# The beginning of a two-layer attention kernel: input rows normalised in groups of four, a second buffer for the modulated rows, and another order of modulation and low part

## What is computed

```python
shift, scale, gate = split(silu(c) @ a_ada_w + a_ada_b, 3)      # one vector c of 1024
u = rms_norm(x, a_norm_g) * (1 + scale) + shift
q, k, v, z = split(u @ a_w_in, 4)                               # 1024 x 4096
q, k = rms_norm per half head of 64
o = (softmax_1(q1 k1) - lam * softmax_2(q2 k2)) @ v             # causal, ALiBi, 8 heads
h = x + gate * ((rms_norm(o) * silu(z)) @ a_w_out)
... # shared k, v from h; then layer 1 the same way with a window of 128
```

## Time and profile before

| | |
|---|---|
| median of 3 runs | 1270.98 us (1269.91 to 1271.34) |
| profiled execution | 1269.83 us, of which the span of the trace is 1268.0 us |
| mean granted TensorE clock | 0.972 of full speed |
| busy: TensorE, VectorE, ScalarE, GpSimd | 91%, 57%, 53%, 14% of the span |
| mean traffic | 85 GB/s |

### The profile page before, as it was taken

One profiled execution on the slowest core, in us unless ns is written; L12 is line 12 of the kernel. 1 busy time (PEld: TensorE's weight loads), 2 busy tenths in 40 slices (PEclk: granted clock), 3 DMA queues, 4 the chain that ended last, 5 costly groups with the idle time before them and its releaser, 6 DMA issues.

```text
span 1268.0 us, 19274 instructions
## 1 busy us (share of the span) xinstructions
PE 1153.3 (91%) x6048; PEld 895.4 (71%) x6048; DVE 724.8 (57%) x2307; ACT 666.6 (53%) x2037; POOL 172.5 (14%) x305
## 2 busy tenths in 40 slices
PE   0657999999999999999996999869999999997998
PEld 0545677777777777777764888758878878786886
DVE  6446667676766677676765354545555545555221
ACT  2356566565656555565654455546666666664110
POOL 3121111110101111010110111031111111110122
PEclk9989999999999999999997999979999999997999
DMA  9411122132222223232224233210111111123342
GB/s 366 168 46 57 55 89 93 64 97 70 84 78 75 86 70 92 69 93 71 90 63 140 96 109 111 68 58 22 48 41 39 39 50 38 42 58 123 116 133 83
DMA packets 52390, 107.42 MB, mean 85 GB/s; under 512 B 5824, under 2 KB 18240, under 8 KB 51264
## 3 DMA queue, kind: packets, MB, share of 16 engines
q1 hardware_dynamic: 52288, 106.18, 26.2%
HBM read 89.38 MB, written 16.78 MB: 84 GB/s over the span
## 4 chain that ended last, share of the span: by engine, by line
PE 81%; DVE 7%; issue 5%; ACT 4%; DMA 2%; POOL 1%; SPq 0%; POOLq 0%; DVEq 0%; ACTq 0%
PE ps_p L512 14%; PE ps_p L514 13%; PE ps_p L513 13%; PE ps_s L544 6%; PE ps_o L591 5%; PE ps_p L690 4%; PE ps_p L691 4%; PE ps_p L692 4%; PE ps_o L659 3%; PE ps_t L615 3%; PE ps_s L643 2%; PE ps_t L675 2%; PE ps_o L714 2%; DVE adabuf L1388 1%; PE ps_o L606 1%
## 5 line engine op out<-in xcount | busy, mean ns | idle before, releaser
L512 PE MATMUL ps_p<-w_hi,u_hi 128*128 128x512 f32 x768 | 338.9, 441 | 0.0
L514 PE MATMUL ps_p<-w_hi,u_lo 128*128 128x512 f32 x768 | 305.4, 398 | 0.0
L513 PE MATMUL ps_p<-w_lo,u_hi 128*128 128x512 f32 x768 | 304.5, 396 | 0.0
L512 PEld LDWEIGHTS ps_p<-w_hi,u_hi 128*128 128x128 f32 x768 | 147.4, 192 | 64.0 <-ACT gbuf L781 28.6
L514 PEld LDWEIGHTS ps_p<-w_hi,u_lo 128*128 128x128 f32 x768 | 146.4, 191 | 33.4
L513 PEld LDWEIGHTS ps_p<-w_lo,u_hi 128*128 128x128 f32 x768 | 148.0, 193 | 17.8
L826 ACT ACTIVATE e<-e,negm 128x256 f32<-128x256 f32 (+7 forms) x128 | 98.2, 768 | 97.9 <-DVE negm L1101 96.9
L1000 DVE TENSOR_TENSOR w_lo<-raw,w_hi 128x512 fp32r<-128x512 f32 x120 | 81.8, 690 | 99.7 <-ACT w_hi L754 99.7
L448 POOL TENSOR_SCALAR gbuf<-gbuf 128x128 f32<-128x128 f32 (+1 forms) x96 | 37.3, 388 | 580.4 <-ACT gbuf L781 580.4
L544 PE MATMUL ps_s<-kT,qT 64*128 64x512 f32 (+3 forms) x384 | 89.4, 542 | 6.4 <-DVE negm L1101 5.4
L754 ACT ACTIVATE w_hi<-raw 128x512 fp32r<-128x512 f32 x128 | 79.3, 629 | 25.0 <-DMA raw<-w_a 19.1
(11 more groups left out here) (169 smaller groups left out, 2051.5 us busy)
## 6 DMA issues: line engine op xcount, KB each, us to landing
adabuf<-ada_w SPq DMA_DIRECT2D x64, 384.0 KB, 3.3
raw<-w_a SPq DMA_DIRECT2D x80, 256.0 KB, 3.5
raw<-w_b SPq DMA_DIRECT2D x48, 256.0 KB, 3.1
ada_in<-ada_w SPq DMA_DIRECT2D x7, 1024.0 KB, 13.2
x_in<-x SPq DMA_DIRECT2D x8, 512.0 KB, 11.9
oa_scratch<-gbuf SPq DMA_DIRECT2D x64, 64.0 KB, 1.6
e<-oa_scratch SPq DMA_DIRECT2D x8, 512.0 KB, 3.9
stage<-x SPq DMA_DIRECT2D x8, 512.0 KB, 5.4
```

The costliest lines, as they stand in the source:

```text
L512: pe.matmul(o, u_hi[:, c, t], w_hi[par][:, c, :], start=(c == 0), stop=False)
L513: pe.matmul(o, u_hi[:, c, t], w_lo[par][:, c, :], start=False, stop=False)
L514: mm = pe.matmul(o, u_lo[:, c, t], w_hi[par][:, c, :], start=False, stop=(c == KD - 1))
```

## The change

The loads of x for tiles 1 to 3 are issued earlier: tile 1 behind tile 0, tiles 2 and 3 between the modulation weights. The groups are ((0, 4), (4, 8)): tiles 0 to 3 are squared before the weight chunks 4 to 7 are split on ScalarE, and VectorE makes their root and normalises all four after the fourth of its weight steps. TensorE transposes tiles 0 and 1 ahead of the sums. `u_mod` gets two buffers, over `oT`, which is used only by the output projections; so tile n waits for the low part of tile n-2. Tiles 0 and 1 are both modulated before the first slot. In the slots, VectorE modulates the next tile right behind the head's normalisation instead of at the slot's end, and makes the low part of tile i at the end of slot i instead of at its start. The memset of `oss`, for which TensorE's first wait (`s_const`) counts, moves to the beginning. GpSimd's normalisations move one slot later. All eight products of the first modulation remain on VectorE and its sums on TensorE.

```diff
         x_in = over(w_at, "x_in", [P, 2, KD, FW])
+        oT_at = nc.sbuf_base + (-nc.sbuf_base) % 32
         oT = sb("oT", [P, 2, D], F32R)
+
+        u_mod = over(oT_at, "u_mod", [P, 2, D])
...
-        x_groups = ((0, 1), (1, 2), (2, 4), (4, 8))
+        ada0_sum = ps_p[:, 0, :]
+
+
+        x_groups = ((0, 4), (4, 8))
...
             load_x(0)
+            load_x(1)
             for c in range(RAW):
                 load_chunk(0, c, w_a[0, :, c, :])
             for c in range(KD - 1):
                 sp.dma_start(ada0_in[:, c, :], ada0_w[c]).then_inc(ada0_loaded[c], 16)
+                if c in (1, 3):
+                    load_x(2 + c // 2)
...
-            for n in range(1, NT):
+            for n in range(4, NT):
                 load_x(n)
...
+                    if is_a and u == 0 and 2 <= i < 5:
+
+                        if i == 2:
+                            pool.wait_ge(n_rs, 2)
+                        for n in ((4, 5), (6,), (7,))[i - 2]:
...
                     part_of_projection(range(0, 3))
-                    if i:
-                        next_rows(0)
+                    next_rows(0)
+                    if i < 3:
+                        next_rows(1)
...
-                    if i:
+                    if i >= 3:
                         next_rows(1)
...
-            rows_of_x(0, 0)
-            rows_of_x(0, 1)
+            for n in range(2):
+                rows_of_x(n, 0)
+                rows_of_x(n, 1)
...
             def x_modulate(n):
                 act.wait_ge(n_tr, 2 * n + 2)
-                at_least(act, u_ready, n)
+                at_least(act, u_ready, n - 1)
...
-                    if isinstance(u, int) and u == 0 and i < NT - 1:
+                    if isinstance(u, int) and u == 0 and 1 <= i < NT - 1:
                         x_modulate(i + 1)
-                        if i < 2:
-                            for n in range(*x_groups[i + 2]):
+                        if i == 1:
+                            for n in range(*x_groups[1]):
                                 x_squares(n)
-                            x_seed(i + 2)
+                            x_seed(1)
...
-            x_squares(0)
+            for n in range(*x_groups[0]):
+                x_squares(n)
             x_seed(0)
...
+            act.wait_ge(s_mod0, 5)
             x_modulate(0)
-            x_squares(1)
-            x_seed(1)
+            x_modulate(1)
...
                 dve.wait_ge(n_tr, 2 * n + 1)
-                at_least(dve, u_ready, n)
-                modulate(x_transposed(n, 0), lambda d: u_mod[:, d * P:(d + 1) * P], 0, M_A_SHIFT, n_umod_d)
+                at_least(dve, u_ready, n - 1)
...
-                    if first and i:
-                        x_low(i)
...
                     if live(2):
                         head_norm(S, s, i2)
+                    if first and 1 <= i < NT - 1:
+                        x_modulate(i + 1)
+                        if i == 1:
+                            x_roots(1)
...
                     split_for(u, i, par, live, units, U_A)
-                    if first and i < NT - 1:
-                        x_modulate(i + 1)
-                        if i == 0:
-                            x_roots(2)
-                            x_normalise(2, 2)
-                        elif i == 1:
-                            x_normalise(2, 3)
-                            x_roots(3)
+                    if first and i >= 2:
+                        x_low(i)
...
             dve.memset(ones[:, :], 1.0)
+            dve.memset(oss[:, :], 0.0).then_inc(s_const, 1)
             dve.memset(var[:, :], 1.0).then_inc(s_const, 1)
...
-            x_roots(0)
-            x_normalise(0, 0)
             acc = adabuf[:, 0:ADA0]
...
+            def ada0(c, step, t, j):
                 dve.wait_ge(ada0_loaded[c], 16)
-                if c == 0:
-                    dve.tensor_scalar(acc, ada0_in[:, 0, :], csil[:, 0:1], None, ALU.mult).then_inc(ada0_used, 1)
-                else:
-                    dve.wait_ge(ada0_used, min(c, KD - 1))
-                    dve.scalar_tensor_tensor(out=acc[:, t], in0=ada0_in[:, j, t], scalar=csil[:, j:j + 1],
-                                             in1=acc[:, t], op0=ALU.mult, op1=ALU.add).then_inc(ada0_used, 1)
-            dve.memset(oss[:, :], 0.0).then_inc(s_const, 1)
+                at_least(dve, ada0_used, min(step, KD - 1))
+                dve.scalar_tensor_tensor(out=acc[:, t], in0=ada0_in[:, j, t], scalar=csil[:, j:j + 1],
+                                         in1=acc[:, t], op0=ALU.mult, op1=ALU.add).then_inc(ada0_used, 1)
+
+            dve.wait_ge(ada0_loaded[0], 16)
+            dve.tensor_scalar(acc, ada0_in[:, 0, :], csil[:, 0:1], None, ALU.mult).then_inc(ada0_used, 1)
+            for c in range(1, KD - 1):
+                ada0(c, c, slice(0, ADA0), c)
+                if c == 3:
+                    x_roots(0)
+                    for n in range(*x_groups[0]):
+                        x_normalise(0, n)
+            for k in range(2):
+                ada0(KD - 1 + k, KD - 1 + k, slice(k * ADA0 // 2, (k + 1) * ADA0 // 2), KD - 1)
...
             x_modulate(0)
             x_low(0)
-            x_roots(1)
-            x_normalise(1, 1)
+            x_modulate(1)
+            x_low(1)
```

More of the change, by code:

```diff
@@ L194, in build @@
         ada_mm = sem("ada_mm")
+        s_mod0 = sem("s_mod0")
         s_mod = sem("s_mod")
@@ L437, in slot @@
                     i2, i3 = (i - 2) % 8, (i - 3) % 8
-                    if is_a and u == 0 and 1 <= i < 4:
-                        if i == 1:
-                            pool.wait_ge(n_rs, 4)
-                        for n in ((4, 5), (6,), (7,))[i - 1]:
+                    if is_a and u == 0 and 2 <= i < 5:
+                        if i == 2:
+                            pool.wait_ge(n_rs, 2)
+                        for n in ((4, 5), (6,), (7,))[i - 2]:
                             pool.tensor_scalar(x_rows(n), x_rows(n), xrs[:, n:n + 1], 1.0, ALU.mult,
@@ L560, in next_rows @@
                     def next_rows(half):
-                        if first and i < NT - 1:
+                        if first and 1 <= i < NT - 1:
                             rows_of_x(i + 1, half)
-                    if first and i == 0:
-                        next_rows(0)
-                        next_rows(1)
                     if live(3):
@@ L742, in _ @@
                 for j in range(k * 8, k * 8 + 8):
-                    mm = pe.matmul(ps_p[:, 0, j:j + 1], adabuf[:, j * P:(j + 1) * P], ones[:, :], start=True, stop=True)
+                    mm = pe.matmul(ada0_sum[:, j:j + 1], adabuf[:, j * P:(j + 1) * P], ones[:, :], start=True, stop=True)
                 mm.then_inc(ada0_mm, 1)
@@ L810, in x_modulate @@
                 act.wait_ge(n_tr, 2 * n + 2)
-                at_least(act, u_ready, n)
+                at_least(act, u_ready, n - 1)
                 for d in range(4, KD):
-                    last = act.activation(u_mod[:, d * P:(d + 1) * P], x_transposed(n, 1)[:, (d - 4) * P:(d - 3) * P],
+                    last = act.activation(u_mod[:, n % 2, d * P:(d + 1) * P], x_transposed(n, 1)[:, (d - 4) * P:(d - 3) * P],
                                           ACT.Identity, scale=smod[:, 0, d:d + 1],
```

30 lines of the change are left out of this document (12 added, 18 removed).

## The result

The changed kernel takes 1250.61 us (1250.21 to 1250.95, 4 runs); the kernel before took 1270.45 (1267.02 to 1271.34, 4 runs) beside it. The ratio is 0.9845 [0.9829, 0.9861]. The gain of 1.4 to 1.7% is clear of the noise, its sign and place are those of the prediction, and it is 1.5 us of span larger than the 17.3 forecast.

The account below looks back on a forecast made before the run. TensorE's own work bounds the kernel after about 135 us, so only earlier standstill can be won: 10.65 + 6.7 = 17.3 us off the profiled 1269.8 gives 1252.5, median 1253.6; range 1250.5 to 1256.5, wider 1250.0 to 1259.0.

Parts of the forecast that it names:

- The start of the modulation: Beginning: first modulation at 45.45 against 42.86, a loss of 2.6 us, since VectorE's weight steps wait for x3 and normalisations.
- The turns: Beginning: VectorE's half steps and GpSimd's splits of chunks 4 to 7 alternate, one split of 1.1 us before each half.
- My lower bound for that case: Beginning, without VectorE and GpSimd alternating: halves end at 37.0 and 38.3, sums at 43.8, 1.4 us later than before.
- First projection: Beginning: TensorE starts it at 49.35 instead of 50.35, no longer queued behind tile 1's transposes.
- The wait at 77.91: TensorE's wait before tile 0's q and k transposes: ends at 68.8, 9.1 us earlier, with some 7 us of standstill left.
- First scores: End of the early part: 10.65 us ahead, with tile 3's transposes half done and the 0.98 us modulation wait covered.
- Slots 3 to 7: VectorE's new order shortens TensorE's waits: 1.85 + 2.05 + 0.85 + 0.8 + 1.2 = 6.7 us gained.
- The loop with the output row as its second gate: From slot 5, q and k transposes also wait for the output row, behind the modulation: period 10.95 us instead of 9.3.
- Rival (a): Only the early gain comes; slots keep 11 to 12 us because TensorE waits for moved VectorE work: 1260.3 us, chance 0.12.
- Rival (b): Early part worse by more GpSimd alternation, or TensorE's low clock costing some 1.6 us per stretch: 1257 us, chance 0.1.
- Rival (c): Beginning: x3's load finishes last, at 41.3 us, holding VectorE; modulation 20 us later, 1273.6 us in all, chance 0.03.
- Rival (d): Whole kernel: nothing measurable, the gain lost again to some later wait; chance 0.01.

Follow-up runs that it names:

- the row-first kernel: Changed kernel, but VectorE's modulation of the next tile stands behind the output row instead of ahead of it: 1248.76 us, ratio 0.9832.
- the kernel without turns: Changed kernel, but GpSimd splits weight chunks 4 to 7 only after VectorE's last half step: 1250.73 us, ratio 0.9846.
- the early squares: Changed kernel, but ScalarE squares tiles 4 to 7, and both engines make their root, ahead of the first modulation: 1244.39 us, ratio 0.9794.
- the beginning alone: Changed kernel with VectorE's old order in the slots (low part at the start, next tile's modulation at the end): 1259.03 us, ratio 0.9908.
- the slots alone: Kernel before, with only the modulation moved forward in slots 2 to 6, low part still at the slot's start: 1270.58 us, ratio 1.0005.
- the later normalisations: Changed kernel, but VectorE normalises tiles 2 and 3 behind its last half step instead of behind the fourth step: 1248.67 us, ratio 0.9838.

## Why the prediction held, step by step

The forecast was 1253.6 and the kernel took 1250.61. Of the 3.0 us, 1.5 is span (18.8 gained, not 17.3). The rest is that I had set the median 1.2 above the profiled execution, and the changed kernel's lies 0.3 below its own. The measured time lies only 0.1 inside the narrower range of 1250.5 to 1256.5. The 1.5 of span is made of errors of both signs: 0.7 too much for the beginning, 0.5 too little for the slots, and 1.7 behind slot 7's start that no term stood for.

- **The start of the modulation: right in kind, 0.6 too small.** Forecast 45.45, measured 46.08. x3's load landed in its turn, 1.1 us later than I had summed (23.9, not 22.8). That wait was part of the chain; the normalisations, at 2.74, were cheaper than the 3.05. The turns were somewhat smaller than I had put them: 1.83 by the kernel without them, where the two splits of 1.1 make 2.2. Late start and smaller turns nearly cancel, and so the halves ended at 38.53 and 40.72 against 38.1 and 40.5. That it is turns, and not a slower VectorE, the kernel without them shows. My lower bound for that case had the sums 1.2 us earlier than the middle value; they moved by 0.87, and the two ends of the range were further apart than the mechanism allows.
- **First projection: 49.35 forecast, 50.05 measured,** the same 0.6 passed on and 0.1 more.
- **The wait at 77.91: 9.1 forecast, 8.2 measured.** Root ready at 64.68 instead of 63.2: 0.7 from above, 0.15 from the nine matmuls, and 0.6 from tile 2's eight transposes, which took 1.91 us in the slow clock where I had put 1.3. That is this execution's clock: with the same instructions up to there they took 1.03 in the kernel with the low part at the slot's start. The step behind it took 5.0 where I had put 5.5 (64.68 to 69.68). That the squares hold this wait is shown by their early version.
- **First scores: 10.65 ahead forecast, 9.93 measured.**
- **Slots 3 to 7: 6.7 forecast, 7.2 measured** (17.1 ahead at 117.60, less 9.9). Step for step: no wait in slot 3 (forecast none), 0.67 (0.65), 2.18 and 2.11 (some 2.1), 1.46 (1.1). The loop with the output row as its second gate was the right model: the row-first kernel takes 1.3 out of each of the two slots.
- **The single waits of the slots, in part luck.** The own work of 8.2, 8.7 and 9.3 belongs to slots 4, 5 and 6, one slot later than the prediction has the first two; a period of 9.3 would then leave 1.1 in slot 4, and one of 10.95 would leave 1.65 in slot 6. The periods came out as 8.71 and 11.21 (80.44 to 89.15, 99.86 to 111.07), so one estimate was 0.6 too long and the other 0.3 too short.
- **What a wait costs beyond its bracket: 0.9, left out.** The brackets of the five slots shrank by 6.25 in all, not 6.7; the other 0.9 is a cost that I had left out. A matmul here starts every 0.23 us but lasts 0.39, and a bracket counts only from the end of the last one. The wait of 1.17 at 103.48 came 1.55 behind the start of the matmul before it; in the changed kernel, without the wait, the same step is 0.23 (99.63 to 99.86). So a wait that goes gives back some 0.2 more than its bracket.
- **The two moves are not additive parts,** as I had treated them: the modulation's move alone, in the kernel before, gives nothing, since there the low part at the slot's start still delays q and k, the row comes 1.3 later, and the longer waits were followed by stretches at the low clock.
- **A term that I didn't have: 1.3 us of clock in slot 7.** The lead grows from 17.1 at 117.60 to 18.4 at 123.62. Windows of the kernel before and of the changed one over the same work:

```profile
134.70:141.00 6.30, 6.28 (x29) 5.12 (x30) 4.63 (x16) 2.92 (x9) 0.19 (x1) 0.73 0.40 117
```

```profile
117.60:124.00 6.40, 6.31 (x36) 4.83 (x38) 4.73 (x16) 3.97 (x12) 0.17 (x1) 1.00 0.39 113
```

Before, the wait of 2.31 at 134.72 was followed by a mean clock of 0.73; now the one of 1.46 is not. With the slots' old order the stretch is back (0.53 from 126.0 to 129.5), and with it the 1.3. The last 0.4 of the lead came late: it is 18.2 at 673.40, 18.5 at 694.17, and 19.1 behind a wait for ScalarE that ends at 811.91 (10.75 where it was 11.31), of which 0.3 is lost again by the end. Whether the change has to do with it is open; no run was made on it.

Rival (a) fell: the low part and the modulation in their new places delay nothing, every slot shortened. Rival (b) fell for this kernel: neither wait of 2.1 was followed by a low stretch in its profile. It was no idle rival, though; in the profiles of the kernel without turns and of that with the early squares it took some 1.6 us. Rival (c) fell: x3 landed at 23.9, far from the break-even of 38.6, so this case doesn't bear on loads that overtake each other. Rival (d) fell with the result.

## What to carry to other kernels

When an instruction moves in an engine's list, follow both the one whose wait it ends and the next gate on the same loop: here the modulation's move paid in time only together with the low part's. A loss inside a chain counts at the consumer only as far as it moves the consumer's first input: 1.83 us on VectorE was 0.87 at a serial sum, while two normalisations taken from ahead of both halves moved the sums by 1.9, and left nothing there for the other edit to win. And look at what an idle engine could do early: ScalarE's four squares, made while it waited, removed a wait of 6.57 us.

## What the runs showed of the hardware

TensorE's clock does not follow the length of the wait alone. The twelve profiles have 16 waits of 2.1 to 3.1 us in the slots. Seven were followed by a stretch at a granted clock near 0.5: 2.18 (early squares), 2.20 (no turns), 2.31 (the kernel before), 2.32 (the beginning alone), 2.97 and 3.04 (the slots alone), 2.98 (low part at the start). Nine were not, with waits from 2.11 to 3.06: 2.18 and 2.11 in the changed kernel, 2.20 and 2.14 with the later normalisations, 3.06 in the same execution as the 2.98. Each such stretch halved the matmuls done in 3.5 us and cost some 1.5 us. None of the 44 waits of 0.65 to 1.78 us in the slots was followed by one within 7 us. I did not find what decides it between 2.1 and 3.1; each kernel has one profiled execution. At the very beginning the clock column is no guide: in the changed kernel it reads 1.00 behind the wait that ends at 50.05, while the nine matmuls there start 0.43 apart, and 0.23 apart from 56.13 on.

VectorE and GpSimd held each other up, short instructions as well as long ones: five steps of VectorE took 11.68 us beside four splits of GpSimd and 9.85 without them, the splits 7.73 and 4.95, and and an instruction of eight columns 0.84 beside a GpSimd instruction, 0.17 without.
